# A new order for the units of a sparse attention on four in-order engines

## The chip, the cores and the metric

The kernel runs on one core of one Trainium2 chip. The metric is the device time of one execution in microseconds (us): before the change 3154.54 us, the median of 3 runs from 3152.24 to 3157.51.

## What is computed

One step of a two-layer encoder, for a prompt of 1024 tokens and for 32 sampled tokens with a cache of 2048 keys. All float32. Cut to the attention, per layer and per block of queries:

```python
def select_and_attend(q, qi, wi, q_pos, k_all, v_all, ki_all, k_pos, topk):   # topk = 256
    dots = einsum('bthd,bsd->bths', qi, ki_all)
    score = einsum('bth,bths->bts', wi, relu(dots))
    score = where((k_pos // 64) <= (q_pos // 64), score, -inf)
    top_val, top_idx = lax.top_k(score, topk)
    kg, vg = gather(k_all, top_idx), gather(v_all, top_idx)
    logits = einsum('btngd,btknd->btngk', qg, kg) * 64 ** -0.5
    p = softmax(where(isfinite(top_val), logits, -inf))
    return einsum('btngk,btknd->btngd', p, vg)
```

Around it each layer has a modulated norm, an input projection, a gated spatial mixer, a convolution mixer, an output projection and a gated feed-forward part with 2816 inner columns.

## The kernel before

Each engine has one queue of instructions, executed in program order; engines wait for one another by semaphores. The kernel is one program of five such queues (SyncE for DMA, GpSimd, ScalarE, TensorE, VectorE), written out by hand. Projections are strips of matmuls with float32 values split in a high and a low part (line 874). The change is in the attention of each layer, which lies from about 455 to 689 us and from 1962 to 2198 us of the span.

The gather is not done. Instead the 256th largest index score of each query is found by a bit-by-bit search (31 steps), and all other keys get a large negative number added to their logits. A search step has three parts: `candidates` on VectorE (L1348: the threshold with one more bit set; it signals `cand_ready`), `count` on ScalarE (L684: how many scores lie above, with one `Sign` activation and its accumulator), `decide` on VectorE (L1360, L1362: keep the bit or not). For the prompt's rows this ran before the attention. For the 32 sampled tokens (`PSRCH`, 2080 keys) it runs inside the attention, beside the prompt's units. `select` on VectorE (L1403 to L1414) makes the mask of one row of queries from its threshold and signals `sel_ready`; `select(n)` belongs to row n+2 and its first logit unit waits for it. Its scratch (`score[:, 0:...]`) is the room of scores no longer needed.

The prompt's 1024 queries are 8 rows of 128 (`QB = 8`). Each row i has

- logit units, "L": for each of 4 pairs of heads and each piece of up to 512 keys of the (i+1) x 128, two 64-row matmul pairs and the mask into a pair of PSUM banks (L1069, L1073), of which VectorE takes the maximum (L1567). 48 units in all: rows 0 to 3 have 4, rows 4 to 7 have 8, of which every second is narrower (128, 256, 384, 512 columns).
- on VectorE, when a row's maxima are there, `diagonals(i)` (L1579): the negated maxima as diagonal matrices in `negmax`, of which there is one; it waits for the scores of the row before.
- score units, "S", one for each block kb of 128 keys, kb = 0 to i: transposed scores with mask and minus the maximum (L1085, L1089, L1091, function `st`), an exponential on ScalarE into one of two `probs` (L778), and the weighted sum `pv` (L1101) into banks 2 and 3. 36 units in all. `pv` of kb = 0 waits for `o_taken` of the row before.
- at the end of a row ScalarE's `reciprocals` (L768, L770) of the sums, and VectorE's `output` (L1593), which signals `o_taken`.

Three pairs of PSUM banks are used in turn (`PLACE`); a unit waits until the unit three places before it was read. The order of the units before is: the L units of row i+1, all of them, then the S units of row i, all of them:

```python
ORDER = [u for i in range(-1, QB) for u in
         [("L", n) for n, x in enumerate(L_UNITS) if x[0] == i + 1] + [("S", n) for n, x in enumerate(S_UNITS) if x[0] == i]]
```

The weighted sum of an S unit comes behind the scores of the next S unit, except that of a row's last S unit, which comes at once. The search steps are placed by two tables: `SEARCH_IN` beside the L units of a row, `SEARCH_BESIDE` beside S units. VectorE does the maxima of row i+1 with its share of steps, then the steps beside S, then `select` of the next mask, then `diagonals(i+1)`. The selection for the sampled tokens comes after row 6 was prepared, and frees the room for the key and value cache, which SyncE loads when `sel_ready` and `v_ones` say so. After the last prompt unit the sampled tokens follow: five pieces of logits, then scores and weighted sums of the same five pieces.

## Time and profile before

| | |
|---|---|
| median of 3 runs | 3154.54 us (3152.24 to 3157.51) |
| the profiled execution | 3157.03 us, its span 3155.3 us |
| TensorE matmuls busy | 2900.4 us, 92% of the span |
| VectorE busy | 1623.1 us, 51% |
| ScalarE busy | 994.8 us, 32% |
| GpSimd busy | 593.0 us, 19% |
| mean granted TensorE clock | 0.965 of full speed |

The profiled execution is one execution; its time is 2.5 us above the median of the runs. In the rows PE is TensorE's matmuls, PEld its weight loads, DVE VectorE, ACT ScalarE, SPq SyncE's queue. "x4" is the number of instructions merged into a row. Matmuls overlap, and the shown ends are modelled, so a unit's time is read from start to start.

### The profile page before, as it was taken

The numbers are of one execution on the slowest core, as the hardware profiler recorded it, in microseconds if no ns is written. First come the engines' busy times: TensorE is split into PE (matmuls) and PEld (weight loads), VectorE is DVE, ScalarE is ACT, GpSimd is POOL, SyncE is SP. The second block draws the span as 40 slices with busy tenths as digits, with TensorE's granted clock in tenths as the row PEclk, the third lists the DMA queues.
The fourth block names the chain that finished last, engine by engine and source line by source line (L and its number), as shares of the span: only waits on it lengthen the run. The fifth ranks groups of instructions, "written<-read, shape, count | busy, mean of one in ns | idle before, by whom it ended". The sixth has DMA issues, their size and how long they took to land.

```text
span 3155.3 us, 43055 instructions
## 1 busy us (share of the span) xinstructions
PE 2900.4 (92%) x16266; PEld 2524.9 (80%) x16266; DVE 1623.1 (51%) x2728; ACT 994.8 (32%) x1258; POOL 593.0 (19%) x254
## 2 busy tenths in 40 slices
PE   6699878999999999999979987889999999999996
PEld 6678753349999999999968876333899999999995
DVE  7647786633343443434554678664335335253355
ACT  1335635623311111111243564563331111111113
POOL 0221220001122122122213123000112212222121
PEclk9999979999999999999989998999899999999998
DMA  8313100011122222222232211001112222222222
GB/s 345 115 46 115 48 35 1 1 34 61 67 100 61 72 81 66 100 67 67 81 123 66 88 68 41 1 1 34 55 65 88 68 79 79 68 86 68 78 79 82
DMA packets 71257, 227.06 MB, mean 72 GB/s; under 512 B 16880, under 2 KB 17136, under 8 KB 69744
## 3 DMA queue, kind: packets, MB, share of 16 engines
q1 hardware_dynamic: 68512, 215.16, 20.1%
q10 hardware_dynamic: 2640, 10.49, 0.8%
q8 instruction: 67, 1.10, 0.1%
q14 instruction: 38, 0.31, 0.0%
HBM read 213.54 MB, written 11.54 MB: 71 GB/s over the span
## 4 chain that ended last, share of the span: by engine, by line
issue 46%; PE 35%; ACT 6%; DVE 5%; POOL 4%; DMA 2%; DVEq 2%; ACTq 0%; POOLq 0%; SPq 0%
PE ps L874 32%; ACT notsel L684 4%; POOL w_lo L552 4%; DMA w_ada<-in_w_ada 2%; PE ps L903 1%; DVE junk L1243 1%; DVE w_ada L1243 1%; DVEq L1350 1%; PE ps L964 1%; DVE notsel L1319 0%; DVE s_cand L1348 0%; DVEq L1253 0%; ACT w_hi L644 0%; DVE swapped L1315 0%; DMA out_y<-hf 0%
## 5 line engine op out<-in xcount | busy, mean ns | idle before, releaser
L552 POOL TENSOR_TENSOR w_lo<-w_raw,w_hi 128x1024 fp32r<-128x1024 f32 x202 | 496.9, 2460 | 2477.6 <-ACT w_hi L644 2477.6
L874 PE MATMUL ps<-u_hi,w_hi 128*128 128x352 f32 (+1 forms) x2112 | 460.7, 326 | 14.6 <-DVE x L1646 12.4
L874 PE MATMUL ps<-u_hi,w_lo 128*128 128x352 f32 (+1 forms) x2112 | 460.4, 326 | 0.0
L874 PE MATMUL ps<-u_lo,w_hi 128*128 128x352 f32 (+1 forms) x2112 | 457.7, 325 | 0.0
L644 ACT CAST w_hi<-w_raw 128x1024 fp32r<-128x1024 f32 x202 | 211.0, 1044 | 592.3 <-PE ps L874 337.9
L874 PEld LDWEIGHTS ps<-u_hi,w_hi 128*128 128x128 f32 x2112 | 364.4, 190 | 17.9 <-issue 15.1
L874 PEld LDWEIGHTS ps<-u_lo,w_hi 128*128 128x128 f32 x2112 | 362.9, 190 | 0.0
L874 PEld LDWEIGHTS ps<-u_hi,w_lo 128*128 128x128 f32 x2112 | 362.6, 190 | 0.0
L684 ACT ACTIVATE notsel<-score,s_cand 128x384 bf16<-128x384 f32 (+3 forms) x248 | 297.4, 1200 | 143.0 <-DVE s_cand L1348 142.8
L1646 DVE SCALAR_TENSOR_TENSOR x<-ps,mod,x 128x704 f32 (+2 forms) x240 | 125.4, 578 | 363.5 <-PE ps L874 356.7
L1243 DVE SCALAR_TENSOR_TENSOR junk<-w_ada,cond_row 128x1024 f32<-128x1024 f32 x124 | 243.7, 1965 | 32.5 <-issue 24.3
L874 PE MATMUL ps<-a_hi,w_hi 128*128 128x352 f32 x1056 | 228.8, 325 | 4.8 <-POOL w_lo L552 2.7
L874 PE MATMUL ps<-a_hi,w_lo 128*128 128x352 f32 x1056 | 227.5, 323 | 0.0
L874 PE MATMUL ps<-a_lo,w_hi 128*128 128x352 f32 x1056 | 227.0, 323 | 0.0
L874 PE MATMUL ps<-h_hi,w_hi 128*128 128x352 f32 x816 | 197.5, 351 | 25.5 <-DVE h_lo L1231 24.3
L1679 DVE COPY up_b<-ps 128x2 f32<-128x2 f32 x44 | 7.0, 159 | 403.5 <-PE ps L874 403.5
L874 PEld LDWEIGHTS ps<-h_hi,w_hi 128*128 128x128 f32 x816 | 137.7, 193 | 73.5 <-issue 59.0
L836 ACT ACTIVATE gate_f<-gate_f,gate_b 128x1024 f32<-128x1024 f32 x88 | 59.9, 728 | 429.7 <-DVE gate_f L1677 429.7
L874 PEld LDWEIGHTS ps<-a_hi,w_hi 128*128 128x128 f32 x1056 | 179.1, 189 | 7.3 <-POOL w_lo L552 5.4
L842 ACT CAST a_hi<-act_f 128x1056 f32 x44 | 47.4, 1077 | 426.2 <-DVE act_f L1684 426.2
L874 PEld LDWEIGHTS ps<-a_hi,w_lo 128*128 128x128 f32 x1056 | 180.9, 188 | 0.0
L874 PEld LDWEIGHTS ps<-a_lo,w_hi 128*128 128x128 f32 x1056 | 179.2, 188 | 0.0
(252 smaller groups left out, 4152.4 us busy)
## 6 DMA issues: line engine op xcount, KB each, us to landing
w_ada<-in_w_ada SPq DMA_DIRECT2D x96, 512.0 KB, 4.9
w_raw<-in_w_up SPq DMA_DIRECT2D x88, 512.0 KB, 3.4
w_raw<-in_w_in SPq DMA_DIRECT2D x34, 512.0 KB, 3.5
cw<-in_convw SPq DMA_DIRECT2D x32, 512.0 KB, 4.6
w_ada<-in_w_ada SPq DMA_DIRECT2D x7, 2048.0 KB, 12.5
w_raw<-in_w_down SPq DMA_DIRECT2D x32, 384.0 KB, 3.1
w_ada<-in_w_ada ACTq DMA_DIRECT2D x5, 2048.0 KB, 12.1
w_raw<-in_w_down SPq DMA_DIRECT2D x32, 320.0 KB, 2.9
```

The costliest lines, as they stand in the source:

```text
L552: nc.gpsimd.tensor_tensor(w_lo[slot][:], w_raw[:], w_hi[slot][:].bitcast(F32), ALU.subtract)\
L644: nc.scalar.copy(w_hi[slot][:], w_raw[:]).then_inc(w_hi_ready.sem, 1)
L684: last = nc.scalar.activation(notsel[0:rows, SC_AT[n]:SC_AT[n + 1]], score[0:rows, SC_AT[n]:SC_AT[n + 1]], ACT.Sign, scale=-1.0, bias=s_ca ...
L836: last = nc.scalar.activation(gate_f[:, t0:t1], gate_f[:, t0:t1], ACT.Silu, bias=gate_b[:, c:c + 1])
L842: nc.scalar.copy(a_hi[:, f, :], act_f[:]).then_inc(a_hi_ready.sem, 1)
L874: last = nc.tensor.matmul(ps[:, bank + t, 0:w], wt[slot][:, kk, :], mv[:, kk, t * TW:t * TW + w], start=(kk == 0 and p == 0), stop=(kk == ...
L903: last = nc.tensor.matmul(ps[:, 6 + e, 0:w], qi[r, pr, i * P:(i + 1) * P], ki[r, c:c + w], start=True, stop=True)
L964: last = nc.tensor.matmul(out[:, half, :], mean_w, src[:, half, :], start=True, stop=True)
L1243: last = nc.vector.scalar_tensor_tensor(out=junk[:] if c == 0 else w, in0=w, scalar=1.0, in1=cond_row[:, c, :], op0=ALU.mult, op1=ALU.mult ...
L1350: dve.drain()
L1646: last = nc.vector.scalar_tensor_tensor(out=dst, in0=src, scalar=mod[:, which, d, c:c + 1], in1=dst, op0=ALU.mult, op1=ALU.add)
L1679: nc.vector.tensor_copy(up_b[:], ps[:, 5, TW:TW + 2])
```

## The change

The order of the units becomes one written-out table, `MIX`, from which all engines take their order. As before, each stretch of it holds the L units of row i+1 and the S units of row i, but mixed: after two or three L units comes an S unit. Numbering the 84 units from 0, row 4's L units (positions 22 to 31) are followed by S units at 32 and 33, row 5's (34 to 43) by 44 to 46, row 6's (47 to 57) by 58 to 60, row 3's (15 to 19) by 20 and 21. The first nine units are as before. The weighted sum of an S unit always comes behind the next unit, whichever kind that is. ScalarE's `reciprocals` come at the unit after a row's last S unit, behind a count if there is one. The 31 search steps are spread evenly over positions 9 to 69 (`STEP_AT`), nearly every second unit (20, 32, 44, 58 are among them); at such a unit VectorE first decides the step before and writes the next candidate, and ScalarE first counts. VectorE's work is now also in the table's order: `select` of the next mask directly after the last maximum of a row, `output` of row i-2 before the second maximum of row i, `diagonals` at a row's last S unit. The sampled selection moves to the first S unit of row 7, behind the output of row 6. The output of row 7 moves behind the second of the five sampled maxima.

```diff
--- before.py
+++ after.py
@@ -69,8 +69,10 @@
 L_UNITS = [(i, b, c, min(512, (i + 1) * P - c)) for i in range(QB) for b in range(4) for c in range(0, (i + 1) * P, 512)]
 S_UNITS = [(i, kb) for i in range(QB) for kb in range(i + 1)]
 N_L, N_S = len(L_UNITS), len(S_UNITS)
-ORDER = [u for i in range(-1, QB) for u in
-         [("L", n) for n, x in enumerate(L_UNITS) if x[0] == i + 1] + [("S", n) for n, x in enumerate(S_UNITS) if x[0] == i]]
+
+MIX = "LLLL" "LLLLS" "LLSLLS" "LLSLLSS" "LLLSLLLSLLSS" "LLLSLLLSLLSSS" "LLSLLSLLSLLSSS" "LLSLLSLLSLLSSSS" "SSSSSSSS"
+ORDER = [(kind, MIX[:at].count(kind)) for at, kind in enumerate(MIX)]
+assert MIX.count("L") == N_L and MIX.count("S") == N_S
 PAIRS = (0, 4, 6)
 PLACE = {u: PAIRS[at % 3] for at, u in enumerate(ORDER)}
 IN_PLACE_BEFORE = {u: ORDER[at - 3] for at, u in enumerate(ORDER) if at >= 3}
@@ -93,9 +95,11 @@
 
 
 SEARCH_AFTER = {6: 2, 7: 4, 8: 4, 9: 4, 10: 4, 11: 3, 12: 3, 13: 2, 14: 2, 15: 2, 16: 1}
-SEARCH_IN = {2: 1, 3: 2, 4: 3, 5: 4, 6: 4, 7: 4}
-SEARCH_BESIDE = {1: 1, 2: 2, 3: 2, 4: 3, 5: 4, 6: 1}
-assert sum(SEARCH_AFTER.values()) == BITS and sum(SEARCH_IN.values()) + sum(SEARCH_BESIDE.values()) == BITS
+assert sum(SEARCH_AFTER.values()) == BITS
+
+L_FIRST = [min(n for n, u in enumerate(L_UNITS) if u[0] == i) for i in range(QB)]
+STEPS_FROM, SEARCH_END = ORDER.index(("L", L_FIRST[2])), ORDER.index(("L", L_FIRST[7] + 6))
+STEP_AT = [ORDER[STEPS_FROM + s * (SEARCH_END - STEPS_FROM) // BITS] for s in range(BITS)]
 LN_EXP = "natural_log_exp_and_others"
 
 ON_ACT = (0, 4, 5, 6)
@@ -778,17 +782,20 @@
                     nc.scalar.activation(probs[t % 2][0:rows, :, 0:w], ps[0:rows, bank:bank + 2, 0:w], ACT.Exp, scale=HD ** -0.5)\
                         .then_inc(p_ready.sem, 1)
 
-                for t, (i, kb) in enumerate(S_UNITS):
-                    if kb == 0:
-                        for _ in range(SEARCH_IN.get(i + 1, 0)):
-                            count(searched, [PSRCH])
-                            searched += 1
-                    if kb < SEARCH_BESIDE.get(i, 0):
+                ended = None
+                for kind, n in ORDER:
+                    if (kind, n) in STEP_AT:
                         count(searched, [PSRCH])
                         searched += 1
-                    exponentials(t, P, PLACE["S", t], 512)
-                    if kb == i:
-                        reciprocals(i, t + 1, 2, 512)
+                    if ended is not None:
+                        reciprocals(S_UNITS[ended][0], ended + 1, 2, 512)
+                        ended = None
+                    if kind == "S":
+                        exponentials(n, P, PLACE["S", n], 512)
+                        i, kb = S_UNITS[n]
+                        if kb == i:
+                            ended = n
+                reciprocals(QB - 1, N_S, 2, 512)
                 assert searched == 2 * BITS
                 for t, (c, w) in enumerate(SAMPLE_CHUNKS):
                     rows = min(P, w)
@@ -1102,16 +1109,16 @@
                                                 stop=(kb == i))
                     last.then_inc(pv_used.sem, 1)
 
+                late = None
                 for kind, n in ORDER:
                     if kind == "L":
                         logits(n)
-                        continue
-                    st(n)
-                    i, kb = S_UNITS[n]
-                    if kb >= 1:
-                        pv(n - 1)
-                    if kb == i:
-                        pv(n)
+                    else:
+                        st(n)
+                    if late is not None:
+                        pv(late)
+                    late = n if kind == "S" else None
+                pv(late)
 
 
                 sample_at = SC_AT[NSRCH - 1]
@@ -1548,31 +1555,19 @@
                     select(m, rank).then_inc(sel_ready.sem, 1)
                     dve.drain()
 
-                def maxima(i, searched):
-
+                def largest(s):
+
+                    i, b, c, w = L_UNITS[s]
                     smax = smax2[:, i % 2]
-                    units = [s for s, u in enumerate(L_UNITS) if u[0] == i]
-                    beat = len(units) // 4
-                    for at, s in enumerate(units):
-                        b, c, w = L_UNITS[s][1:]
-                        if at == len(units) // 2 and i >= 2:
-
-                            output(i - 2, 2, P, (i - 2) * P, (i - 1) * P)
-                        if at % beat == 0 and at // beat < SEARCH_IN.get(i, 0):
-                            if at:
-                                decide(searched + at // beat, PSRCH, NSRCH)
-                            candidates(PSRCH, NSRCH)
-                        dve.wait_ge(s_ready.sem, s_ready.at(l, s + 1))
-                        bank = PLACE["L", s]
-                        nc.vector.tensor_reduce(smax[:, c // 512, :].rearrange("p (n b) -> p n b", n=2)[:, :, b],
-                                                ps[:, bank:bank + 2, 0:w], AX.X, ALU.max).then_inc(s_taken.sem, 1)
-                    dve.drain()
-                    if (i + 1) * P > 512:
-                        nc.vector.tensor_tensor(smax[:, 0, :], smax[:, 0, :], smax[:, 1, :], ALU.max)
+                    dve.wait_ge(s_ready.sem, s_ready.at(l, s + 1))
+                    bank = PLACE["L", s]
+                    nc.vector.tensor_reduce(smax[:, c // 512, :].rearrange("p (n b) -> p n b", n=2)[:, :, b],
+                                            ps[:, bank:bank + 2, 0:w], AX.X, ALU.max).then_inc(s_taken.sem, 1)
+                    if b == 3 and c + w == (i + 1) * P:
                         dve.drain()
-                    if i in SEARCH_IN:
-                        decide(searched + SEARCH_IN[i], PSRCH, NSRCH)
-                    return searched + SEARCH_IN.get(i, 0)
+                        if (i + 1) * P > 512:
+                            nc.vector.tensor_tensor(smax[:, 0, :], smax[:, 0, :], smax[:, 1, :], ALU.max)
+                            dve.drain()
 
                 def spread(n, of):
 
@@ -1595,37 +1590,48 @@
                                                        recip[:, n, 0:4 * w].rearrange("p (b t) -> p b t", b=4), ALU.mult)
                     last.then_inc(o_taken.sem, 1)
 
-                searched = maxima(0, searched)
-                diagonals(0)
-
-                dve.wait_ge(ki_stored.sem, ki_stored.at(l, 16))
-                settle(dve)
-                start_search(PSRCH, NSRCH)
-                for i in range(QB):
-                    if i + 1 < QB:
-                        searched = maxima(i + 1, searched)
-                        for _ in range(SEARCH_BESIDE.get(i, 0)):
-                            candidates(PSRCH, NSRCH)
+                for at, (kind, n) in enumerate(ORDER):
+                    if (kind, n) in STEP_AT:
+                        if (kind, n) != STEP_AT[0]:
                             searched += 1
                             decide(searched, PSRCH, NSRCH)
-                        if i + 1 == QB - 1:
-                            assert searched == 2 * BITS
-                            finish_search(PSRCH, NSRCH)
+                        candidates(PSRCH, NSRCH)
+                    if at == SEARCH_END:
+                        searched += 1
+                        decide(searched, PSRCH, NSRCH)
+                        assert searched == 2 * BITS
+                        finish_search(PSRCH, NSRCH)
+                    if kind == "L":
+                        i = L_UNITS[n][0]
+                        if n == L_FIRST[i] + 1 and i >= 2:
+                            output(i - 2, 2, P, (i - 2) * P, (i - 1) * P)
+                        largest(n)
+                        if n + 1 == N_L or L_UNITS[n + 1][0] != i:
+                            if i == 0:
+                                diagonals(0)
+                                dve.wait_ge(ki_stored.sem, ki_stored.at(l, 16))
+                                settle(dve)
+                                start_search(PSRCH, NSRCH)
+                            elif 3 <= i < QB - 1:
+
+                                assert SC_AT[i - 1] >= WIDTHS[i - 1]
+                                select(i - 1, score[:, 0:WIDTHS[i - 1]]).then_inc(sel_ready.sem, 1)
+                                dve.drain()
+                    else:
+                        i, kb = S_UNITS[n]
+                        if (i, kb) == (QB - 1, 0):
+                            output(QB - 2, 2, P, (QB - 2) * P, (QB - 1) * P)
                             select(PSRCH, rank_samp).then_inc(sel_ready.sem, 1)
                             dve.drain()
                             nc.vector.memset(vcache[:, :, :, HD:P], 1.0).then_inc(v_ones.sem, 1)
-                        elif i >= 2:
-
-                            select(i, score[:, 0:WIDTHS[i]]).then_inc(sel_ready.sem, 1)
-                            assert SC_AT[i] >= WIDTHS[i]
-                            dve.drain()
-                        diagonals(i + 1)
-                for i in range(QB - 2, QB):
-                    output(i, 2, P, i * P, (i + 1) * P)
+                        if kb == i and i + 1 < QB:
+                            diagonals(i + 1)
                 for c, (c0, w) in enumerate(SAMPLE_CHUNKS):
                     dve.wait_ge(ss_ready.sem, ss_ready.at(l, c + 1))
                     bank = SAMPLE_PAIRS[c % 2]
                     nc.vector.tensor_reduce(smax_s[:, :, c], ps[:, bank:bank + 2, 0:w], AX.X, ALU.max).then_inc(ss_taken.sem, 1)
+                    if c == 1:
+                        output(QB - 1, 2, P, (QB - 1) * P, QB * P)
                 dve.drain()
                 nc.vector.tensor_reduce(smax_s[:, :, N_SL], smax_s[:, :, 0:N_SL], AX.X, ALU.max)
                 dve.drain()
```

## Rows read from the trace of the kernel before

**Rows 1.** Windows of both attentions: each engine's busy time, clock, DMA.

```profile
455.50:689.00 233.50, 206.70 (x720) 77.58 (x722) 137.79 (x260) 114.80 (x113) 0.00 (x0) 0.95 0.07 21
1962.20:2198.30 236.10, 209.79 (x720) 78.54 (x720) 137.63 (x260) 114.97 (x112) 0.00 (x0) 0.93 0.07 21
```

**Rows 2.** Waits of TensorE, layer 0's attention: us, times, longest.

```profile
PE ps L1101 <- ACT probs L778: 14.8, 6, 3.1
PE ps L1069 <- DVE smax L1567: 11.1, 7, 4.1
```

**Rows 3.** Timeline of TensorE, first units: start, us, work, idle before.

```profile
461.64 0.80 PE L1069 MATMUL ps<-k,q 64*128 64x128 f32 x4 [4.09 <-DVE smax L1567]
...
469.73 1.23 PE L1069 MATMUL ps<-k,q 64*128 64x256 f32 x4 [2.51 <-DVE smax L1567]
```

**Rows 4.** Timeline of TensorE, single units.

```profile
494.08 1.13 PE L1069 MATMUL ps<-k,q 64*128 64x512 f32 x4
...
495.68 1.13 PE L1069 MATMUL ps<-k,q 64*128 64x512 f32 x4
...
506.94 1.95 PE L1101 MATMUL ps<-probs,vaug 128*128 128x512 f32 x4 [3.14 <-ACT probs L778]
...
641.72 1.13 PE L1085 MATMUL ps<-q,k 64*128 64x512 f32 x4
...
643.69 1.88 PE L1101 MATMUL ps<-probs,vaug 128*128 128x512 f32 x4
645.50 1.13 PE L1085 MATMUL ps<-q,k 64*128 64x512 f32 x4
```

**Rows 5.** Timeline of VectorE: decision, candidate, first and last instruction of selections.

```profile
484.78 0.16 DVE L1360 TENSOR_TENSOR s_keep<-s_cnt,s_need 128x1 uint32<-128x1 f32 x1
...
485.32 0.21 DVE L1348 TENSOR_SCALAR s_cand<-s_thr,s_bit 128x1 uint32<-128x1 uint32 x1
...
509.38 0.88 DVE L1403 TENSOR_SCALAR_CACHE_REDUCE score<-score,s_tmp 128x640 f32<-128x640 f32 x1
...
514.63 1.23 DVE L1579 SCALAR_TENSOR_TENSOR negmax<-con,smax 128x1024 fp32r<-128x1024 f32 x1
...
603.68 1.28 DVE L1403 TENSOR_SCALAR_CACHE_REDUCE score<-score,s_tmp 128x1024 f32<-128x1024 f32 x1
...
611.11 1.22 DVE L1579 SCALAR_TENSOR_TENSOR negmax<-con,smax 128x1024 fp32r<-128x1024 f32 x1
...
638.31 2.37 DVE L1403 TENSOR_SCALAR_CACHE_REDUCE rank_samp<-score,s_tmp 32x2080 f32<-32x2080 f32 x1
```

**Rows 6.** Groups of VectorE, layer 0's attention: busy us, mean ns, idle.

```profile
L1567 DVE TENSOR_REDUCE smax<-ps 128x2 f32<-128x1024 f32 (+3 forms) x48 | 44.0, 954 | 19.0 <-PE ps L1073 17.8
...
L1593 DVE TENSOR_TENSOR mix<-ps,recip 64x512 f32<-64x512 f32 x14 | 9.5, 679 | 4.8 <-ACT recip L770 4.7
```

**Rows 7.** Timeline of ScalarE: reciprocal (two), count, exponential.

```profile
478.04 1.02 ACT L768 ACTIVATE recip<-ps 64x1024 f32<-64x1024 f32 x1 [2.07 <-PE ps L1101]
479.13 1.06 ACT L770 ACTIVATE recip<-recip 64x1024 f32<-64x1024 f32 x1
...
485.57 2.03 ACT L684 ACTIVATE notsel<-score,s_cand 32x2080 bf16<-32x2080 f32 x1 [3.38 <-DVE s_cand L1348]
...
505.77 1.02 ACT L778 ACTIVATE probs<-ps 128x1024 f32<-128x1024 f32 x1
```

**Rows 8.** Windows around one long wait of TensorE; granted clock third from last.

```profile
631.00:635.00 4.00, 0.95 (x4) 0.38 (x3) 1.79 (x5) 3.88 (x4) 0.00 (x0) 0.99 0.00 0
635.00:638.00 3.00, 3.00 (x6) 0.98 (x6) 2.77 (x6) 0.18 (x1) 0.00 (x0) 0.50 0.00 0
```

**Rows 9.** Timeline of SyncE, the value cache loads.

```profile
654.06 2.42 SPq L507 DMA_DIRECT2D vcache<-in_vcache  x2
```

**Rows 10.** DMA issues from 640 to 720: KB each, us to landing.

```profile
vcache<-in_vcache SPq DMA_DIRECT2D x2, 512.0 KB, 5.8
```

**Rows 11.** Timeline of TensorE, sampled part.

```profile
693.83 1.13 PE L1128 MATMUL ps<-kcache,q_samp 64*128 64x512 f32 x4 [1.72 <-DVE smax_s L1628]
```

## The prediction

> **What bounds the kernel now.** I read the share of busy time first (TensorE 92% of the span, table above), then the windows of the two stretches that the change touches, then who TensorE waits for in them, then the timelines of the three engines. The attention of layer 0 takes 233.5 us with TensorE busy 206.7 us, that of layer 1 takes 236.1 with 209.8 [rows 1]. VectorE (137.8) and ScalarE (114.8) are far from full. So the most that a new order can win is TensorE's 26.8 us of idle time a layer plus some lost clock. The waits split that: 14.8 us for probabilities, before weighted sums; 11.1 us before logit units for VectorE's maxima [rows 2]. Of the latter 4.09 + 2.51 = 6.6 us fall in the first nine units [rows 3], where the new table has the old order. 26.7 - 6.6 = 20.1 us a layer can go. The reader should see in the timelines that every old wait is one exponential behind two or three search counts on ScalarE, at most 3.1 us long.
>
> **What does not change.** The same 48 logit (L) and 36 transposed-score (S) units, matmuls, reductions, counts and selections are issued. An L unit of 512 columns takes 495.68 - 494.08 = 1.60 us of TensorE, a narrow one 0.65 (128 columns) to 0.95 (256; both estimates in proportion to columns, with a fixed part); an S unit with its weighted sum takes 645.50 - 641.72 = 3.78, of which 643.69 - 641.72 = 1.97 is the scores and 1.81 the sum [rows 4]. So the sum of the new stage is the work plus the stalls that the three in-order queues make.
>
> **The new stalls: a walk through the table.** I walk the units at full clock with these prices. VectorE: decision to next candidate 485.32 - 484.78 = 0.54; a selection from 514.63 - 509.38 = 5.25 us (640 columns) to 611.11 - 603.68 = 7.43 (1024), 5.96 and 6.69 between them [rows 5]; a reduction 0.95 on average (0.4 to 1.2 by width), an output 2 x 0.68 = 1.4 [rows 6]. ScalarE: candidate to count 485.57 - 485.32 = 0.25; a count 2.03, 2.15 until VectorE can decide; a reciprocal 1.02 + 1.06 = 2.1; start of an exponential to start of its weighted sum 506.94 - 505.77 = 1.17 [rows 4, 5, 7].
>
> (a) Row ends. For rows 3 to 6 VectorE takes the last maximum of the row and goes straight into the selection of the next row's mask. The unit after that L is an S unit, and in all four rows it carries a search step (positions 20, 32, 44, 58 of the table). ScalarE's queue has the count ahead of that unit's exponential, and the count waits for a candidate which VectorE writes only after the selection. Price for row 5: reduction and combine 1.1, selection 6.7, decision and candidate 0.8, count 2.1, exponential to sum 1.2: 11.9 us. TensorE has two S units' scores to do meanwhile, 3.95, and then stands before the late weighted sum: 7.9 us. Rows 3, 4, 6 by the same line: 6.7, 6.9, 8.9. Sum 30.4 us. In the old order the selection came after all counts of the block, so nobody waited behind it.
>
> (b) Row starts. The output of the row before is now ahead of the second L's maximum, and waits for the reciprocal, which waits for the last weighted sum. From the end of that sum: 0.2 + 2.1 + 1.4 + 0.5 (narrow reduction) + 0.8 + 2.15 + 1.2 = 8.3 us until the first weighted sum of the next S row; TensorE has 0.65 + 1.6 + 1.97 + 0.65 = 4.9 of work. Stalls 3.3 (row 4), 3.0 (row 5), 0.7, 0.3, 0.3 (rows 6, 7, 3, with other steps): 7.6 us.
>
> (c) Single exponentials behind one count of the unit before: 1.3 and 1.6 in row 2, 1.1, 0.9, 1.5, 1.7 in rows 4 to 7; and 1.8 where the first weighted sum of row 7 waits for the output of row 6. Sum 9.8 (9.9 by the rounded terms).
>
> Together 47.7 us, in place of 20.1: +27.6. The walk is at full clock; the old stretch holds 206.7 us of busy time against 202.4 in the walk, 4.3 of it slow-clock time. Walk against measurement: 455.6 to 712.3 for 455.6 to 688.9, +23.4 us.
>
> (d) Clock. After the idle 4 us from 631 the granted clock was 0.50 in the next 3 us, 0.99 before [rows 8]: a spell costs about 1.7 us of work. Four stalls of 7 to 9 us, two of 3 and the small ones give 4 to 6 spells: I take 8 us; bounds 4.3 (nothing beyond the old) and 18 (each of the long stalls costs two spells, each of the others one). For the Trainium skill (TensorE: Matmul & The Clock Gate, Part 1: The HAM clock gate) half rate is the default state, which idling brings back and activity lifts. By that rule every long stall is followed by a slow spell, four for certain, 6.8 us by the row's 1.7; the row agrees.
>
> (e) The sampled selection moves from unit (6,1) to unit (7,0), behind the output of row 6. It hides: from its start to the last cache load landed was 654.06 + 2.42 + 5.8 - 638.31 = 24.0 us [rows 5, 9, 10]; from the end of that output TensorE has 8 weighted sums and 6 scores left, 8 x 1.81 + 6 x 1.97 = 26.3 us. Margin 2.3 us; without it, 0 to 5 us a layer (the upper end if the loads take twice their 5.8 us).
>
> (f) The last output goes behind two of the sampled maxima: 1.72 us of idle time goes [rows 11], about 0.9 of it is left after the next wait. -1 us.
>
> (g) The search's own count (31 steps) and VectorE's sum don't change: 0 there, since neither is full [rows 1].
>
> **Sum.** +23.4 + 8 - 1 = +30.4 a layer, two layers +60.8; layer 1 of before already holds 236.1 - 233.5 = 2.6 us more lost clock, so +58. Against the profiled execution, 3157.0 (span 3155.3): 3215. The median of the runs is 2.5 lower, 3154.5, so 3212; rounding down a little because small waits in the walk may overlap: 3210.
>
> **Rivals.**
> 1. *The interleaving works as an interleaving.* The L units give TensorE work under the exponentials, the old waits of up to 3.1 us vanish and nothing takes their place: -20 a layer and 1 to 4 of clock: 3154.5 - 44 = 3110. For it: 14.8 us of probability waits sit where S follows S at once [rows 2]. Against it: the order of the queue on VectorE at the row ends. It decides at whether the candidate is written before the selection; by the code it is not. The Trainium skill (Perfetto Trace Analysis, Optimization Strategy) holds that interleaving phases with different busiest engines may pay; by that rule this rival's time is the one to expect, and rows 1 speak against it only in that TensorE is the busiest in both phases. Chance 0.06.
> 2. *The stalls come but small*: the row ends cost half (15 us) since VectorE is ahead of my walk, row starts as computed: 15 + 7.6 + 5 = 28 against 20 + 4 of clock: +4 a layer at most, -1 at least: 3153 to 3163. Chance 0.05, half of it within the bound of no change.
> 3. *Worse than the walk*: clock at its upper bound and the cache loads late: +10 and +5 a layer beyond: 3240. For it: four idle stretches longer than any now. Chance 0.12.
> 4. *It does nothing* because TensorE's work bounds the stage: that would need stalls of 24 a layer; against it (a). Held in 2.
>
> **How the numbers follow.** Forecast 0.77, rival 3 0.12, rival 2 0.05, rival 1 0.06. Slower: 0.77 + 0.12 + half of rival 2 = 0.91; same 0.03; faster 0.06. What this kernel's measurement can tell from no change is about 0.2%, 6 us. Range: low end where the walk is 12 us a layer too high (half of (b) and (c), and clock at 4.3): 3210 - 24 = 3186; high end rival 3's 3240.
>
> **What would show it.** In the profile after: four TensorE waits of 6 to 9 us a layer for probabilities, each with ScalarE's count waiting over 5 us for the candidate, and VectorE in a selection; the attention windows at about 264 us instead of 233.5; sampled part unchanged or 1 us shorter; all else the same. Wrong would be: no wait over 4 us (rival 1 or 2), or a new wait for the cache loads at the sampled part (e).

## The result and the profile after

The changed kernel takes 3215.08 us, the median of 4 runs from 3214.9 to 3217.22, for 3153.39 us before on the same chip: ratio 1.0195, 95% interval 1.0177 to 1.0212. It is slower, by 62 us; forecast were 3210 us and a range of 3186 to 3240. Its profiled execution has a span of 3213.2 us.

First the windows of the two attentions, as in [rows 1]: length, then busy time of TensorE, its weight loads, VectorE, ScalarE.

```profile
452.10:719.90 267.80, 214.74 (x708) 78.98 (x720) 139.02 (x260) 114.06 (x112) 0.00 (x0) 0.90 0.06 18
1991.10:2258.90 267.80, 214.81 (x706) 78.96 (x718) 138.95 (x260) 114.05 (x112) 0.00 (x0) 0.90 0.06 18
```

The third number from the end is TensorE's granted clock, as a share of full speed. The attentions take 267.8 us each for 233.5 and 236.1. VectorE and ScalarE are as busy as before to 1.5 us. TensorE's busy time grew by 8 and 5 us with the same instructions, and the granted clock fell from 0.95 and 0.93 to 0.90. (A dozen of the matmul records are missing in each of these windows, so busy time reads a little low; below, idle time is taken from the gaps that the timeline shows.) The waits of TensorE in the first window, as in [rows 2]:

```profile
PE ps L1108 <- ACT probs L782: 42.2, 13, 8.8
PE ps L1076 <- DVE smax L1564: 6.6, 2, 4.0
...
PE ps L1108 <- DVE mix L1588: 1.9, 1, 1.9
```

Each line gives us in total, times, and the longest. Waits for maxima fell from 11.1 to 6.6 us, which are the first units' [rows 3]. Waits for probabilities rose from 14.8 to 42.2, the longest from 3.1 to 8.8. TensorE's timeline shows where they are: all at a weighted sum, the four long ones (6.36, 6.49, 7.50, 8.84) at the second S unit behind a row's last L unit, where the weighted sum of the first is due.

```profile
509.93 3.78 PE L1108 MATMUL ps<-probs,vaug 128*128 128x512 f32 x4 [6.36 <-ACT probs L782]
...
525.93 3.50 PE L1108 MATMUL ps<-probs,vaug 128*128 128x512 f32 x4 [3.11 <-ACT probs L782]
...
549.30 3.77 PE L1108 MATMUL ps<-probs,vaug 128*128 128x512 f32 x4 [6.49 <-ACT probs L782]
...
565.00 1.96 PE L1108 MATMUL ps<-probs,vaug 128*128 128x512 f32 x4 [3.04 <-ACT probs L782]
...
588.14 3.78 PE L1108 MATMUL ps<-probs,vaug 128*128 128x512 f32 x4 [7.50 <-ACT probs L782]
...
636.23 3.78 PE L1108 MATMUL ps<-probs,vaug 128*128 128x512 f32 x4 [8.84 <-ACT probs L782]
...
693.57 1.98 PE L1108 MATMUL ps<-probs,vaug 128*128 128x512 f32 x4 [1.87 <-DVE mix L1588]
```

The end of row 5 on the two other engines, first VectorE, then ScalarE. (L1410 to L1421 is the selection, L1355 writes the candidate, L688 is the count, L782 the exponential.)

```profile
576.55 0.69 DVE L1564 TENSOR_REDUCE smax<-ps 128x2 f32<-128x512 f32 x1 [1.61 <-PE ps L1080]
...
577.60 1.15 DVE L1410 TENSOR_SCALAR_CACHE_REDUCE score<-score,s_tmp 128x896 f32<-128x896 f32 x1
...
583.04 1.15 DVE L1421 SCALAR_TENSOR_TENSOR notsel<-score,s_tmp,notsel 128x896 bf16<-128x896 f32 x1
...
584.82 0.21 DVE L1355 TENSOR_SCALAR s_cand<-s_thr,s_bit 128x1 uint32<-128x1 uint32 x1
```

```profile
585.07 2.03 ACT L688 ACTIVATE notsel<-score,s_cand 32x2080 bf16<-32x2080 f32 x1 [9.52 <-DVE s_cand L1355]
...
587.09 1.90 ACT L782 ACTIVATE probs<-ps 128x1024 f32<-128x1024 f32 x2
588.90 2.01 ACT L688 ACTIVATE notsel<-score,s_cand 32x2080 bf16<-32x2080 f32 x1
```

VectorE takes the row's last maximum at 576.6 and selects from 577.6 to 584.2. Only then does it decide and write the candidate (584.8). ScalarE has waited 9.5 us for it with the count at the head of its queue; the two exponentials behind that count start at 587.1, though their scores were done at about 578.5 and 580.6. TensorE goes on at 588.1. Then the clock, in windows around this stall (granted clock third from last):

```profile
582.00:586.00 4.00, 0.00 (x0) 0.00 (x0) 2.86 (x6) 0.93 (x1) 0.00 (x0) 0.71 0.00 0
586.00:590.00 4.00, 1.86 (x2) 0.84 (x3) 0.74 (x4) 4.00 (x5) 0.00 (x0) 0.50 0.00 0
590.00:594.00 4.00, 4.00 (x8) 0.96 (x7) 0.00 (x0) 1.01 (x2) 0.00 (x0) 0.51 0.00 0
594.00:598.00 4.00, 4.00 (x14) 1.68 (x13) 1.22 (x1) 1.02 (x1) 0.00 (x0) 1.00 0.00 0
```

After 7.5 us without a matmul the granted clock is 0.50 to 0.51 until 594, the level of 1.2 GHz and not that of 2.4; I call such a stretch a slow spell. The units behind the stall, read from start to start, with the weighted sum of 588.14 first:

```profile
591.85 2.08 PE L1092 MATMUL ps<-q,k 64*128 64x512 f32 x4
...
594.77 1.88 PE L1108 MATMUL ps<-probs,vaug 128*128 128x512 f32 x4
596.58 1.13 PE L1076 MATMUL ps<-k,q 64*128 64x512 f32 x4
```

The weighted sum takes 3.7 us (588.14 to 591.85) for 1.8, the scores behind it 2.9 for 2.0 [rows 4], the next sum 1.8 again: this stall costs 2.9 us more than its length. For the other three it is 2.7, 1.9 and 2.8 by the same reading.

What lies around the attentions: from the first sampled logits to the first transposed sampled scores 9.1 us pass in both layers, for 10.4 and 11.6 before. The first attention starts 3.4 us earlier than in the profile of before, through nothing that was changed. 34.3 + 31.7 (the windows) - 1.3 - 2.4 - 3.4 - 1.0 (the rest) = 57.9 us is the difference of the spans.

### The profile page after: what moved, and what is told of

The parts are those of the page before. It is cut to its first block, busy times and chain, and to the rows that moved or that the text cites. A ratio compares the mean times of both kernels' runs of the same rounds, so it can differ in the third digit from the quotient of the medians.

```text
span 3213.2 us, 43031 instructions
## 1 busy us (share of the span) xinstructions
PE 2910.8 (91%) x16242; PEld 2526.5 (79%) x16266; DVE 1626.0 (51%) x2728; ACT 993.3 (31%) x1258; POOL 594.1 (18%) x254
## 4 chain that ended last, share of the span: by engine, by line
issue 47%; PE 35%; ACT 5%; DVE 5%; POOL 4%; DVEq 2%; DMA 2%; ACTq 0%; POOLq 0%; SPq 0%
PE ps L881 33%; ACT notsel L688 4%; POOL w_lo L556 3%; DMA w_ada<-in_w_ada 1%; PE ps L910 1%; DVE w_ada L1250 1%; DVE junk L1250 1%; DVEq L1357 1%; PE ps L971 1%; DVE notsel L1326 0%; DVEq L1260 0%; DVE s_cand L1355 0%; ACT w_hi L648 0%; DMA out_y<-hf 0%; DVE swapped L1322 0%
## 5 line engine op out<-in xcount | busy, mean ns | idle before, releaser
L688 ACT ACTIVATE notsel<-score,s_cand 128x384 bf16<-128x384 f32 (+3 forms) x248 | 297.4, 1200 | 211.4 <-DVE s_cand L1355 211.0
L1108 PE MATMUL ps<-probs,vaug 128*128 128x512 f32 x288 | 155.6, 668 | 88.6 <-ACT probs L782 84.6
```

Of the source, the lines that this page charges most:

```text
L688: last = nc.scalar.activation(notsel[0:rows, SC_AT[n]:SC_AT[n + 1]], score[0:rows, SC_AT[n]:SC_AT[n + 1]], ACT.Sign, scale=-1.0, bias=s_ca ...
L1108: last = nc.tensor.matmul(ps[:, 2 + n, :], vaug[:, kb, n, :], probs[t % 2][:, n, :], start=(kb == 0), stop=(kb == i))
```

## The experiments

The ratios are to the kernel before, run beside each on the same chip (medians 3152.8 to 3155.5 us). Most are edits of the changed kernel; gains against it use its 3215.1 us of the section above, so they hold to some 2 us. Stalls are of layer 0, those of layer 1 agree within 0.5 us where both were read.

### The selection ahead of the candidate, tested from three sides

**Steps off the row ends.**

```diff
+ROW_END = [at for at, u in enumerate(ORDER) if u[0] == "S" and ORDER[at - 1][0] == "L" and ORDER[at - 1][1] + 1 in L_FIRST[4:]]
+STEP_AT = [ORDER[ORDER.index(u) - 1] if ORDER.index(u) in ROW_END else u for u in STEP_AT]
```

> The changed kernel with the four search steps that stand at the first S unit after a row's last L unit (positions 20, 32, 44, 58) moved one unit earlier, so that VectorE writes the candidate before the row's last maximum and before the selection. Theory (the selection stands ahead of a candidate that ScalarE's exponential waits behind): the four stalls a layer of 6.4, 6.5, 7.5 and 8.8 us go; 0.8 and 1.8 come back behind the counts at positions 46 and 60, and some 7 us of slow clock go with them: 29.2 - 2.6 + 7 = 34 us a layer, 3215 - 68 = 3147 us (3135 to 3160). Rival (the mixed order itself is slow: TensorE waits for VectorE's maxima or for a work-bound VectorE whatever the steps do): the stalls only move to another unit, 3200 to 3215. Rival (the late sampled selection is what costs): no gain, 3215.

Measured: 3146.74 us, ratio to before 0.9982 (0.9972 to 0.9992). The expected number was 3147. TensorE's timeline:

```profile
506.43 1.13 PE L1078 MATMUL ps<-k,q 64*128 64x512 f32 x4 [0.75 <-DVE notsel L1423]
...
518.55 3.75 PE L1110 MATMUL ps<-probs,vaug 128*128 128x512 f32 x4 [3.23 <-ACT probs L784]
...
539.29 1.13 PE L1078 MATMUL ps<-k,q 64*128 64x512 f32 x4 [1.32 <-DVE notsel L1423]
...
551.97 3.75 PE L1110 MATMUL ps<-probs,vaug 128*128 128x512 f32 x4 [3.21 <-ACT probs L784]
...
577.96 1.98 PE L1110 MATMUL ps<-probs,vaug 128*128 128x512 f32 x4 [0.51 <-ACT probs L784]
...
616.21 1.98 PE L1110 MATMUL ps<-probs,vaug 128*128 128x512 f32 x4 [1.76 <-ACT probs L784]
```

No stall is left at a row end but the two foreseen behind later counts (0.51 and 1.76 us) and two new, small ones, before the masks of rows 4 and 5 (0.75, 1.32). The two at the row starts stay (3.23, 3.21). Both stalls of 3.2 us at the row starts are now followed by a slow spell (3.75 us for the weighted sum). Moving four of 31 search steps by one unit is worth 68 us.

**The selection behind the step.**

```diff
                             decide(searched, PSRCH, NSRCH)
                         candidates(PSRCH, NSRCH)
+                    if mask_of is not None:
+                        select(mask_of, score[:, 0:WIDTHS[mask_of]]).then_inc(sel_ready.sem, 1)
+                        dve.drain()
+                        mask_of = None
...
-                                select(i - 1, score[:, 0:WIDTHS[i - 1]]).then_inc(sel_ready.sem, 1)
-                                dve.drain()
+                                mask_of = i - 1
```

> The changed kernel with the selection of the next mask moved on VectorE from directly after a row's last maximum to behind the step of the following S unit; the steps stay where they are. Theory: the candidate comes 5 to 7 us earlier, but the row's last reduction still stands ahead of it; by the walk 1.4, 1.0, 1.3 and 1.4 us of stall stay at positions 20, 32, 44, 58, and 0.5 and 1.4 come at 46 and 60. 29.2 - 7.0 + 7 of clock = 29 us a layer: 3157 us (3145 to 3170). If it were the step's place that costs and not the selection ahead of it, this would gain nothing: 3215. If the delayed selection held up the next row's first logit unit (it has three to four units of room): over 3180.

Measured: 3160.50 us, ratio 1.0023 (1.0013 to 1.0032). The steps are where they were; what went is only the selection ahead of them. So it was the order of the two on VectorE, and not the place of the step by itself. The waits for probabilities are 15 small ones:

```profile
PE ps L1108 <- ACT probs L782: 18.8, 15, 3.2
...
PE ps L1076 <- DVE notsel L1421: 1.6, 2, 1.2
```

**The exponential ahead of the count.** At S units ScalarE does the exponential first:

```diff
-                    if (kind, n) in STEP_AT:
+                    if (kind, n) in STEP_AT and kind == "L":
                         count(searched, [PSRCH])
...
                         exponentials(n, P, PLACE["S", n], 512)
...
+                        if (kind, n) in STEP_AT:
+                            count(searched, [PSRCH])
+                            searched += 1
```

> The changed kernel with ScalarE doing the exponential of an S unit ahead of the count that stands at the same unit, nothing else. Theory: the exponential at a row's end no longer waits for the candidate, but that of the next S unit stands behind the same count, so TensorE gets one weighted sum and one unit more (3.4 to 4 us) before it stands: the four stalls fall from 6.4, 6.5, 7.5, 8.8 to 3.3, 3.0, 4.0, 5.0, and 1.3, 1.1 and 1.4 elsewhere go or shrink to 0.5: 16 us a layer and a few us of clock: 3215 - 36 = 3179 us (3165 to 3190). Rival (VectorE's lateness alone makes the stall, whoever is first on ScalarE): no gain, over 3205.

Measured: 3171.34 us, ratio 1.0056 (1.0039 to 1.0073). 8 us better than expected and still 16 us above before: the next exponential stands behind the same count, and the longest wait is 5.1 us.

```profile
PE ps L1111 <- ACT probs L782: 22.5, 10, 5.1
```

### The row starts

```diff
-                        if n == L_FIRST[i] + 1 and i >= 2:
+                        if n == L_FIRST[i] + (2 if i in (4, 5) else 1) and i >= 2:
                             output(i - 2, ...)
```

> The changed kernel with the output of the row before placed ahead of the third maximum instead of the second in rows 4 and 5 alone, which puts it behind the step of that unit. Theory (at a row's start the candidate waits behind the output, which waits for the reciprocal): the two stalls of 3.1 and 3.0 us a layer go and one spell of slow clock of 1.6 us: 7.7 us a layer, 3215 - 15 = 3200 us (3196 to 3206). Rival (they are exponentials behind a count that is late anyway, since the decision before it waits for the count two units back): under 3 us in all, 3212 to 3215.

Measured: 3199.02 us, ratio 1.0145 (1.0128 to 1.0162).

```profile
523.58 1.96 PE L1108 MATMUL ps<-probs,vaug 128*128 128x512 f32 x4 [0.56 <-ACT probs L782]
...
558.61 1.96 PE L1108 MATMUL ps<-probs,vaug 128*128 128x512 f32 x4 [0.25 <-ACT probs L782]
```

The waits of 3.11 and 3.04 us are 0.56 and 0.25. The rival of 3212 falls.

> The first and the third of these together: steps off the row ends, and the output behind the step in rows 4 and 5. Theory: the gains add, 68 + 15: 3132 us (3120 to 3145), 20 us under the kernel before the change. Rival (the row start's stall is absorbed once the row end before it is short, or grows): 3147 or more.

Measured: 3129.54 us, ratio 0.9923 (0.9907 to 0.994). The two gains add (68 + 16 = 84, measured 86).

### What the mixing itself is worth

> The changed kernel without the 31 search steps of the sampled tokens inside the attention (the sampled threshold is not searched for; everything else is done). It shows what the mixed order is worth when no count stands ahead of an exponential. Theory: of 44.1 us of stalls a layer after the first units some 6 stay (0.8 and 1.2 where the masks of rows 4 and 5 come late, 1.9 before the first weighted sum of row 7, the rest small), and 11 of slow clock go: 3215 - 2 x 49 = 3117 us (3108 to 3130). Rival (VectorE's maxima bound the mixed order): over 3150.

> The kernel before the change without the same 31 search steps. Theory: its 14.8 us of waits for exponentials go and most of the 4.5 us of waits for maxima, with 3 to 6 us of slow clock: 3154 - 2 x 19 = 3116 us (3108 to 3125), the same as the mixed order without the steps within 6 us, so that mixing itself wins nothing and the steps' places are all that counts. Rival (the mixing has a worth of its own, hidden by the row ends): this one is 15 us or more slower than the mixed order without the steps.

Both kernels leave out the search of the sampled tokens' threshold, 31 steps a layer, and with it the right mask for these tokens; the rest is done. (The numbers of signals, changed to match, are not shown.)

```diff
-STEP_AT = [ORDER[STEPS_FROM + ...] for s in range(BITS)]      # in the changed kernel
+STEP_AT = []
-SEARCH_IN = {2: 1, 3: 2, ...}; SEARCH_BESIDE = {1: 1, ...}    # in the kernel before
+SEARCH_IN = {}; SEARCH_BESIDE = {}
```

Measured: mixed 3107.00 us (ratio 0.9848, 0.9831 to 0.9864), old order 3104.96 us (0.9842, 0.9822 to 0.9862). The intervals overlap: without the steps, mixing wins nothing. In the attentions alone it loses some 4 us a layer (213.0 and 212.8 us mixed, 209.2 and 208.6 in the old order, from the first logits to the first sampled logits), which the shorter sampled part gives back in part. Both kernels are about 10 us under what I expected: from 475 us to the end of layer 0's attention the granted clock is 1.00 in both, so that all of the slow clock behind the first units went, of which I had counted on a part. The waits, mixed first, then the old order:

```profile
PE ps L1075 <- DVE smax L1563: 6.1, 2, 3.6
PE ps L1075 <- DVE notsel L1420: 2.0, 2, 1.3
PE ps L1107 <- DVE mix L1587: 1.6, 1, 1.6
```

```profile
PE ps L1068 <- DVE smax L1566: 6.6, 2, 4.1
...
PE ps L1100 <- ACT probs L778: 1.1, 1, 1.1
```

In the old order the first units' 6.6 us and 1.1 us are all that is left of over 0.3 us within the prompt's units: an S unit of 3.78 us of TensorE covers a 1 us exponential already. The mixed order has waits for masks (2.0) and for the output (1.6) instead.

**The old table with the new rules**, that is `MIX` put back to all L units, then all S units:

```diff
-MIX = "LLLL" "LLLLS" "LLSLLS" ...
+MIX = "".join("L" * sum(x[0] == i + 1 for x in L_UNITS) + "S" * (i + 1) for i in range(-1, QB))
```

> The changed kernel with the table of the units put back to the order of before (all L units of a row, then all S units of the row before), while the steps stay spread evenly and the selections, outputs and weighted sums stay where the change put them. Theory (the places of the steps and selections cost, not the mixing): the steps fall on the second S unit behind the selection in rows 3 and 4 and on the first in rows 5 and 6, stalls 2.8, 3.1, 7.9, 8.9; the output ahead of the second maximum stops four rows of L units by 1.8 each; 6 us of others: 38 us against 44 a layer, 3200 us (3185 to 3215). Rival (the mixing is what costs): back to 3155 to 3165. Rival (the mixing helps and this makes it worse): over 3220.

Measured: 3212.37 us, ratio 1.0182 (1.0165 to 1.0199), 12 us over the expected number, within its range. The order can be put back and 59 of the 62 us stay. They are not the same 59: the waits for probabilities are 28.6 us for 42.2 and the longest are longer, and the waits for maxima are 18.4 for 6.6. The row ends cost 3.4, 3.5, 7.9 and 10.9 us.

```profile
PE ps L1108 <- ACT probs L782: 28.6, 7, 10.9
PE ps L1076 <- DVE smax L1564: 11.4, 9, 3.6
PE ps L1092 <- DVE smax L1564: 7.0, 6, 3.6
```

### The two other parts

**The sampled selection early.**

```diff
                         if (i, kb) == (QB - 1, 0):
                             output(QB - 2, ...)
+                        if (i, kb) == (QB - 2, 3):
                             select(PSRCH, rank_samp).then_inc(sel_ready.sem, 1)
```

> The changed kernel with the sampled selection moved back from the first S unit of row 7 to the fourth S unit of row 6 (position 72), ahead of the diagonals of row 7, so that only its late place is undone. Theory (the late place costs nothing and even keeps VectorE free for the diagonals): the selection and the fill, 15.5 us, now stand ahead of the diagonals of row 7; TensorE has 11 us of work, so the first scores of row 7 wait 5.6 us and a slow spell of 1.7 us follows: +7 a layer, 3215 + 14 = 3229 us (3220 to 3236). Rival (the late selection is part of what made the change slow, by late cache loads or a late first sampled piece): faster than the changed kernel, under 3212.

Measured: 3231.72 us, ratio 1.024 (1.0223 to 1.0257). The late place is worth 17 us in this schedule. With the early place the first scores of row 7 wait for the diagonals:

```profile
PE ps L1092 <- DVE negmax L1574: 5.3, 1, 5.3
```

**The weighted sums one unit behind, in the kernel before.**

```diff
...
-                    if kb >= 1:
-                        pv(n - 1)
-                    if kb == i:
-                        pv(n)
...
+                    if late is not None:
+                        pv(late)
+                    late = n if kind == "S" else None
...
```

> The kernel before the change with the weighted sums always one unit behind, nothing else: a row's last weighted sum comes after the next unit. Theory: 1.1 us a layer is won behind the first S unit and 1.6 lost before the first weighted sum of row 7, whose output now has only one S unit's scores as cover: 3155 us, no difference that can be measured (3150 to 3160). Rival (this part is what pays or costs): over 6 us either way.

Measured: 3180.62 us, ratio 1.0086 (1.0069 to 1.0103), 28 us more than before where I expected none. The trace points at a reason. Row 4's first L units, ScalarE, VectorE, TensorE:

```profile
518.33 1.02 ACT L768 ACTIVATE recip<-ps 64x1024 f32<-64x1024 f32 x1 [5.99 <-PE ps L1101]
519.42 1.06 ACT L770 ACTIVATE recip<-recip 64x1024 f32<-64x1024 f32 x1
520.38 2.01 ACT L684 ACTIVATE notsel<-score,s_cand 32x2080 bf16<-32x2080 f32 x1
```

```profile
522.52 0.16 DVE L1360 TENSOR_TENSOR s_keep<-s_cnt,s_need 128x1 uint32<-128x1 f32 x1 [3.12 <-ACT notsel L684]
```

```profile
524.87 0.49 PE L1069 MATMUL ps<-k,q 64*128 64x128 f32 x4 [2.10 <-DVE smax L1567]
```

The row's last weighted sum is now behind an L unit that waits for its mask. The reciprocal starts at 518.3 for 514.4 before, the count behind it at 520.4, VectorE's decision waits 3.1 us for the count, with two maxima behind the decision, and TensorE waits 2.1 us for PSUM. To test that:

> The kernel before the change with the weighted sums one unit behind (3180.6 us, expected 3155), and now ScalarE's first count of a row ahead of the reciprocals of the row before instead of behind them. Theory for the miss: a row's last weighted sum now comes behind a logit unit that itself waits for the mask; the reciprocal starts 3.9 us later (518.3 for 514.4), the first count stands behind it, VectorE's decision waits 3.1 us for the count with two maxima behind it, and TensorE stands 1.5 to 2.1 us for them in each of rows 4 to 7. With the count first these waits go: some 7 us a layer and 2 of clock, 3163 us (3156 to 3170); 1.9 us a layer stay at row 7 and 1.6 before the masks. Rival (the late sum itself, or the late output, holds the banks): 3176 or more.

```diff
-                        for _ in range(SEARCH_IN.get(i + 1, 0)):
+                        for step in range(SEARCH_IN.get(i + 1, 0)):
                             count(searched, [PSRCH])
                             searched += 1
+                            if step == 0 and i:
+                                reciprocals(i - 1, t, 2, 512)
...
```

Measured: 3158.79 us, ratio 1.0009 (0.9996 to 1.0022), 22 of the 28 us back. The reason holds. The 6 us left are about what two new waits cost in two layers, 1.9 us for a mask (0.2 before) and 1.9 for the output of row 6 (none before). The waits for maxima, the first units' 6.6 among them, fall from 17.4 + 1.9 to:

```profile
PE ps L1073 <- DVE smax L1571: 8.5, 6, 4.1
```

### The best version

The version with both repairs (3129.5 us), with the exponential first at S units, and in TensorE's loop

```diff
+                    if kind == "S" and S_UNITS[n] == (QB - 2, QB - 2):
+                        pv(n)
+                        late = None
```

> The version with steps off the row ends and the later output in rows 4 and 5 (3129.5 us), and two more edits: ScalarE does the exponential ahead of the count at S units, and the weighted sum of row 6's last S unit is done at once, so that its reciprocal and output are ready for row 7. Theory: stalls of 1.3, 1.1, 1.8, 1.4 and 1.9 us a layer go, about 1.5 comes back where the next exponential stands behind the count: 6 us a layer, 3117 us (3110 to 3124). Rival (ScalarE is late only by its sum of work between two S units): 3127 or more.

Measured: 3112.97 us, ratio 0.9869 (0.9852 to 0.9885), 40 us under before and 102 under the changed kernel. It is within 8 us of the kernels that leave the steps out.

```profile
PE ps L1081 <- DVE smax L1572: 6.6, 2, 4.1
PE ps L1113 <- ACT probs L784: 4.7, 6, 1.5
```

## Why the prediction was right

By the steps of the prediction, under its letters, in layer 0, us:

| step | predicted | measured |
|---|---|---|
| (a) row ends 3, 4, 5, 6 | 6.7, 6.9, 7.9, 8.9 | 6.36, 6.49, 7.50, 8.84 |
| (b) row starts 4, 5, others | 3.3, 3.0, 1.3 | 3.11, 3.04, 0.45 |
| (c) singles and output of row 6 | 9.8 | 8.3 |
| sum of stalls after the first units | 47.7 | 44.1 |
| (d) slow clock and rest, beyond the walk | 8 | 14.7 |
| length of the attention | 264.7 | 267.8 |
| (f) sampled part | -1 | -1.3 (layer 1: -2.4) |

(a) right in place, cause and size; three experiments agree (the step moved, the selection moved, ScalarE's order swapped), each near the time forecast for it. (b) right: moving the output takes just these two waits.

(c) The sum is 1.5 us lower. Which price was too long is not shown.

(d) The mis-sized term. I took 1.7 us a spell from one stall of 3 us [rows 8]. There the weighted sum took 3.2 us for 1.8, and the scores behind it, up to 639.91, 2.3 for 2.0:

```profile
634.41 3.23 PE L1101 MATMUL ps<-probs,vaug 128*128 128x512 f32 x4 [3.05 <-ACT probs L778]
637.58 1.50 PE L1085 MATMUL ps<-q,k 64*128 64x512 f32 x4
```

Behind a stall of 6 to 9 us the spell covers all of the weighted sum and, in three of four, part of the next unit, and costs 1.9 to 2.9 us, 10.3 in all; the 3.1 us stall at 525.93 adds 1.6. Measured over the whole stretch it is 14.7 (267.8 less 6.6 and 44.1 of idle time, less the 202.4 of the walk); the 2.8 us between are not assigned to a place. The upper bound of 18 held it.

The 202.4 us do not follow from the prices given: the L units by [rows 4] and the estimates are 61.3 us, the S units 136.1, together 197.4. The 5 us between are close to the 4.4 that the first nine units lost in the profile of before (455.56 to 474.91, less 6.6 of waits, is 12.75 us, for 8.4 by the prices), where the granted clock is about 0.5 for most of the time, before and after; so the walk seems to have taken these units as measured, and not at full clock. They are the same before and after, and the difference is untouched.

By luck the errors cancel. In a layer, +6.7 in (d) and -3.6 of stalls leave the attention 3.1 us longer than forecast. The forecast for the profiled executions was +58 us, and 57.9 was measured; but the attentions grew by 66.0 us for 60 forecast, the sampled part shrank by 3.7 for 2, and 4.4 us went elsewhere (the 3.4 of the earlier start and the rest of 1.0). The step from 3212 to 3210, for small waits that may overlap, pointed the wrong way.

The granted clock was 0.50 to 0.51 during the weighted sum behind each of the four long stalls, which took 3.8 us. The Trainium skill (TensorE: Matmul & The Clock Gate, Part 1: The HAM clock gate) says that idling brings the slow clock back, and the trace agrees in all four. The price of a spell comes from the rows.

(e) right: the last cache loads were issued from 709.29 to 711.86 and took 6.0 us, so they landed by about 717.9. TensorE waits for all cache loads before its first sampled logits, which start at 719.87 with no wait. The margin was 2.0 us for 2.3 forecast.

```profile
709.29 2.57 SPq L511 DMA_DIRECT2D vcache<-in_vcache  x2
```

```profile
vcache<-in_vcache SPq DMA_DIRECT2D x2, 512.0 KB, 6.0
```

(f) is right in layer 0. In layer 1, 1.1 of the 2.4 us are slow clock that the profile of before had there and that of after had not.

Two readings of the prediction need a correction. Not every old wait for probabilities stood behind two or three counts: the first, 1.1 us at the first S unit, has no count ahead of it and stays when the steps are left out. And [rows 1] show whole attentions, not L and S units apart, so they do not show which engine is busiest in each. [rows 4] and the walk's prices do: an L unit of 512 columns is 1.60 us of TensorE and up to 1.2 of VectorE, an S unit 3.78 of TensorE and 1.0 of ScalarE.

What the prediction did not see: the weighted sum one unit behind can be a cost of its own. In (b) it is there as a later reciprocal, but I put (b) down to the output's place. In the old order the same edit alone costs 28 us, through a reciprocal that is 3.9 us later; what it costs in the mixed order was not tested.

The rival that mixing pays falls: TensorE is the busiest in both kinds of units, and with the steps out the two orders take the same time. The Trainium skill (Perfetto Trace Analysis, Optimization Strategy) says that interleaving may help where the most contended engine changes from one regime to the next. Here it does not change, so this case does not contradict it.

Left open: how the 62 us divide among all parts. The row ends account for 68 us taken alone, the row starts for 16 (these two add), and the late selection for -17; the rest of the parts were not taken out one by one, and with the old table the same total comes from other waits.

## What to carry to other kernels

In a ring of in-order queues an instruction's place counts for what stands behind it on every engine: a selection of 5 to 7 us put one place ahead of a 0.2 us candidate held ScalarE's exponentials and TensorE, 6.4 to 8.8 us each time, and moving four candidates by one place gave 68 us. Mixing two kinds of work won nothing here, where TensorE bounds both. Take the side work out first and see whether a gap is left that mixing could fill. In this kernel a stall of TensorE of over 6 us costs its length and 2 to 3 us of slow clock behind it.

## What was not expected of the hardware

Whether a short stall of TensorE is followed by a slow spell changes from case to case, with the same length and the same place. In the kernel before, the first long wait of row 2's weighted sums is 3.14 us in layer 0, and the sum behind it takes its 1.95 us [rows 4]. The same wait in layer 1 is followed by a slow one:

```profile
2013.35 3.19 PE L1101 MATMUL ps<-probs,vaug 128*128 128x512 f32 x4 [3.13 <-ACT probs L778]
```

In the changed kernel the sums behind waits of 3.11 and 3.04 us took 3.50 and 1.96, in layer 1 3.46 and 1.96. Even 1.87 us of idle time can be followed by a spell: the first weighted sum of row 7 takes 1.98 us in the changed kernel (693.57 above) and, behind the same wait, this in the kernel with the old table:

```profile
693.82 3.68 PE L1108 MATMUL ps<-probs,vaug 128*128 128x512 f32 x4 [1.87 <-DVE mix L1588]
```

Stalls of 6.3 to 8.9 us were all followed by one, in both layers of the changed kernel: the weighted sum took 3.76 to 3.78 us each of eight times.
